# Another order of the tensors in SBUF: the arena of hidden rows ahead of constants and split activations

## The reference

```python
def first_block(...):
    proj = rmsnorm(h, g) @ w_in                  # q, k, v, u, y
    h += concat(dilated attention, bidirectional RG-LRU) @ w_out
    h += cross attention to 256 memory rows      # w_cq, w_ck, w_cv, w_co
    hid = square(relu(rmsnorm(h, g) @ w_mlp_in)) # 1024 x 4096
    h += hid @ w_mlp_out                         # 4096 x 1024
    return rmsnorm(h, g)

def second_block(...):                           # two layers
    z = rmsnorm(x) @ w_in                        # four branches and four gates
    x += (gated sum of MLA, FNet, differential attention, HGRN2) @ w_out
    x += (silu(g) * u) @ w_down                  # w_gate_up: 1024 x 5632, w_down: 2816 x 1024
```

## Time and profile before

| | |
|---|---|
| median of 3 runs | 1296.85 us (1294.33 to 1297.41) |
| the profiled execution | 1295.53 us |
| its span, first to last instruction | 1293.7 us |
| TensorE matmul busy | 1265.9 us (98%) |
| TensorE weight loads busy | 1178.1 us (91%) |
| VectorE busy | 862.2 us (67%) |
| ScalarE busy | 652.5 us (50%) |
| GpSimd busy | 114.4 us (9%) |
| granted TensorE clock, mean | 0.994 |

### The profile page before, as it was taken

How to read it: one execution, slowest core, us unless ns; L and a number is a source line. 1 busy time by engine, 2 the same in 40 slices (tenths; PEclk the granted TensorE clock), 3 DMA queues, 4 the chain that set the end, 5 groups by cost and what they waited for, 6 DMA issues and landing times.

```text
span 1293.7 us, 22072 instructions
## 1 busy us (share of the span) xinstructions
PE 1265.9 (98%) x9208; PEld 1178.1 (91%) x9208; DVE 862.2 (67%) x1194; ACT 652.5 (50%) x1049; POOL 114.4 (9%) x152
## 2 busy tenths in 40 slices
PE   8999999999999999998999999999999999999998
PEld 8998999988788989997999998888899988999986
DVE  6897667644466675998656553667577996655543
ACT  5896655543368464342544443556552434544432
POOL 1100000000000000661000000000003810000000
PEclk8999999999999999999999999999999999999999
DMA  9543445555535323442555555433343325455552
GB/s 368 204 163 115 180 135 192 196 185 180 188 101 193 131 99 131 164 152 84 189 189 176 190 196 185 165 139 136 112 145 131 134 96 196 165 191 174 187 196 98
DMA packets 30324, 211.77 MB, mean 164 GB/s; under 512 B 3344, under 2 KB 3728, under 8 KB 5264
## 3 DMA queue, kind: packets, MB, share of 16 engines
q1 hardware_dynamic: 29936, 210.22, 45.5%
q10 hardware_dynamic: 288, 0.14, 0.0%
HBM read 209.29 MB, written 1.05 MB: 163 GB/s over the span
## 4 chain that ended last, share of the span: by engine, by line
PE 74%; DVE 13%; ACT 6%; issue 5%; DMA 1%; SPq 0%; DVEq 0%; ACTq 0%
PE bank L508 72%; DVE w_lo L1625 3%; ACT w_hi L1125 2%; DVE W L1599 2%; DMA ring<-weight_pieces 1%; ACT W L1125 1%; PE bank L608 1%; PE bank L843 1%; DVE xs L2125 1%; DVE W L1585 1%; DVE junk L2123 1%; DVE W L2105 1%; DVE W L1586 1%; DVE W L1617 0%; DVE stat L1558 0%
## 5 line engine op out<-in xcount | busy, mean ns | idle before, releaser
L1625 DVE TENSOR_TENSOR w_lo<-ring,w_hi 128x2048 fp32r<-128x2048 f32 x183 | 422.5, 2309 | 283.9 <-ACT w_hi L1125 283.5
L1125 ACT ACTIVATE w_hi<-ring 128x1024 fp32r<-128x1024 f32 (+1 forms) x368 | 366.2, 1046 | 241.9 <-PE bank L508 226.2
L508 PE MATMUL bank<-x_hi,w_hi 128*128 128x256 f32 x1840 | 267.2, 284 | 2.4 <-ACT w_hi L1125 2.4
L508 PE MATMUL bank<-x_hi,w_lo 128*128 128x256 f32 x1840 | 261.5, 281 | 1.0 <-DVE w_lo L1625 0.9
L508 PE MATMUL bank<-x_lo,w_hi 128*128 128x256 f32 x1840 | 254.8, 280 | 0.0
L508 PEld LDWEIGHTS bank<-x_hi,w_hi 128*128 128x128 f32 x1840 | 237.0, 189 | 5.7 <-issue 2.4
L508 PEld LDWEIGHTS bank<-x_hi,w_lo 128*128 128x128 f32 x1840 | 236.5, 188 | 2.3 <-DVE w_lo L1625 1.7
L508 PEld LDWEIGHTS bank<-x_lo,w_hi 128*128 128x128 f32 x1840 | 233.6, 188 | 0.0
L508 PE MATMUL bank<-W 128*128 128x128 f32 (+4 forms) x716 | 110.7, 327 | 8.3 <-ACT W L1125 4.8
L508 PEld LDWEIGHTS bank<-W 128*128 128x128 f32 (+3 forms) x716 | 87.8, 187 | 21.5 <-issue 12.3
L508 PE MATMUL bank<-w_lo,hid_hi 128*128 128x512 f32 x304 | 78.5, 394 | 0.0
(11 more groups left out here) (257 smaller groups left out, 1238.0 us busy)
## 6 DMA issues: line engine op xcount, KB each, us to landing
ring<-weight_pieces SPq DMA_DIRECT2D x191, 1024.0 KB, 4.8
const<-constants SPq DMA_DIRECT2D x1, 1376.5 KB, 8.9
W<-x_features SPq DMA_DIRECT2D x4, 256.0 KB, 5.2
ring<-weight_pieces SPq DMA_DIRECT2D x2, 512.0 KB, 6.0
h<-x SPq DMA_DIRECT2D x2, 512.0 KB, 11.9
W<-rg_weights SPq DMA_DIRECT2D x1, 1024.0 KB, 9.7
xs<-mem_features SPq DMA_DIRECT2D x1, 1024.0 KB, 11.4
oT<-mem SPq DMA_DIRECT2D x1, 1024.0 KB, 11.4
```

Of the source, the lines that this page charges most:

```text
L508: return nc.tensor.matmul(out, lhsT, rhs, start=first, stop=last)
L1125: return nc.scalar.activation(out, in_, ACT.Copy, scale=scale)
L1625: v.tensor_tensor(w_lo[:, q % SPLITS, 0:n], raw(pp)[:, 0:n], w_hi[:, q % SPLITS, 0:n].bitcast(F32), ALU.subtract).then_inc(s_weight_low, 1)
```

## The change

Four groups of allocations change their order; nothing else does. Before: `ring`, `w_hi`, `w_lo`, `const`, `vec`, `row`, `h`, `xs`, `x_hi`, `x_lo`, `oT`, `W`, `junk`, ... After: `ring`, `w_hi`, `w_lo`, `h`, `xs`, `oT`, `W`, `const`, `vec`, `row`, `x_hi`, `x_lo`, `junk`, ... So `ring`, `w_hi`, `w_lo`, `junk`, `stat` and `rrow` stay where they are, and all others move. The arena with the hidden rows starts 57,344 bytes behind the start of `w_hi`, a multiple of 1024.

```diff
         w_hi = sb("w_hi", [P, SPLITS, PIECE], F32R)
         w_lo = sb("w_lo", [P, SPLITS, PIECE], F32R)
-        const = sb("const", [P, C_SIZE])
-        vec = sb("vec", [P, V_SIZE])
-        row = sb("row", [P, R_SIZE])
         h = sb("h", [P, TT, D])
         xs = sb("xs", [P, TT, D])
-        x_hi = sb("x_hi", [P, KT, S], F32R)
-        x_lo = sb("x_lo", [P, KT, S], F32R)
         oT = sb("oT", [P, KT, S])
         W = sb("W", [P, ARENA])
         arena0 = nc.sbuf_base - 4 * ARENA
...
         mem_lo = nc.alloc_sbuf_tensor_at("mem_lo", [P, KT, S], F32R, offset=arena0 + 4 * A_U)
+        const = sb("const", [P, C_SIZE])
+        vec = sb("vec", [P, V_SIZE])
+        row = sb("row", [P, R_SIZE])
+        x_hi = sb("x_hi", [P, KT, S], F32R)
+        x_lo = sb("x_lo", [P, KT, S], F32R)
         junk = sb("junk", [P, D], BF16)
```

## The result

The changed kernel takes 1300.56 us (median of 5, 1299.92 to 1301.06), the kernel before 1294.91 us (median of 5, 1293.5 to 1297.41): ratio **1.0039**, 95% interval 1.0027 to 1.0051. It is slower by 0.4%. The forecast was no change, 1296.5 us.

What follows compares the result with a forecast made beforehand. TensorE's matmul count times start-to-start pace was taken as the bound, 996 of 1293.7 us. All terms of the change were taken as 0, giving 1296.5 us, between 1295.53 (profiled) and 1296.85 (median); range 1271 to 1309.

Steps and rivals of the forecast that it cites:

- Other engines: Accesses of engines besides TensorE to the moved tensors: covered by the matmuls, no row making their effect other than 0.
- the feature matmuls, 192 to 160: 5520 matmuls with activations moving, remainder by 512 from 192 to 160: pace stays at 117.8 ns, 0 us.
- the bound above, +26 us: Upper limit for the 5520 feature matmuls: one more step like 113 to 118 ns, +4.8 ns each.
- rival C: Slower, equal or off-line places collide more: feature +4 us, token +3, hidden rows +2.4, total 1306 us; chance 0.26.
- Token matmuls, 320 to 352: 1152 matmuls with weights moving and activations stationary, remainder by 512 from 320 to 352: taken as 0 us.
- the bound above, +3 us: Upper limit for the 1152 token matmuls: all at 118 ns, instead of half at 113 and half at 118.
- Down matmuls, 320 to 0: 912 matmuls of 512 columns on hidden rows, remainder 320 to 0: stay at 233.3 ns, 0 us; bounds -16 and +6.
- rival B: Only the down stage gets faster, 224 to 228 ns, -5 to -8 us, 1290 us; chance 0.15 including small feature gains.
- The remark on mem_hi: Memory rows mem_hi, at a multiple of 128, were the slower of their pair; given on the down term's open sign.
- C's parts on feature and token matmuls: Slower case's terms: feature matmuls +0.7 ns each, +4 us; token matmuls always at 118 ns, +3 us.
- C's part on the hidden rows: Slower case's term for the down matmuls: 236 ns, which a pass could reach by 1%, +2.4 us.
- C's reason: Slower case's mechanism: TensorE's moving read and weight load meet at the same place more often.

Runs made afterwards that it cites:

- e1: Kernel before, with 32 unused bytes ahead of x_hi and 480 ahead of W, so only the split activations change remainder; ratio 1.0073, 1305.15 us.
- e2: Kernel before, with 192 unused bytes ahead of W, so only the hidden rows change remainder, to 0; ratio 0.993, 1287.16 us.
- e3: Kernel before, with 32 unused bytes ahead of ring, so every tensor from ring on shifts and all distances stay; ratio 1.0004.
- e4: Kernel before, with 384 unused bytes ahead of x_hi and 64 ahead of W, exchanging feature and token remainders; ratio 0.9916, 1285.07 us.
- a2: Changed kernel with 480 unused bytes ahead of x_hi, restoring the activations' old remainder; ratio 0.9963 to the kernel before, 1290.24 us.
- a1: Changed kernel with 96 unused bytes ahead of x_hi, feature remainder 64; ratio 0.9908 to the kernel before, 1283.09 us.
- s3: Kernel before, with 128 unused bytes ahead of x_hi and 96 ahead of W: feature remainder 64, hidden rows 32; ratio 0.9972.
- s1: Kernel before, with 192 unused bytes ahead of x_hi and 128 ahead of W: feature remainder 0, hidden rows 128; ratio 1.0091, 1305.94 us.

## Why the prediction was wrong

**What held.** TensorE sets the time, the number of matmuls times their pace carries 77% of the span, and the only question was whether the remainders of the distances count. The distances and remainders worked out from the sizes were right, and so was the suspicion that the remainder and not the distance matters. (They are those from the start of the moving tensor to that of the stationary one; the text names the opposite direction.) Other engines: 0, as forecast. The range held the time.

**Step that failed: the feature matmuls, 192 to 160, "I take 0".** It interpolated between two rows, 128 (memory rows, 118.0 ns) and 192 (117.8). Remainder 160 lies between them and has 119.94. Two things were wrong in it. The pace isn't a smooth function of the remainder, so neighbours don't bound a place between them. And the 118.0 ns wasn't the pace of 128: 24 of the 56 memory matmuls move mem_lo, which is at 192. The next row of mem_hi alone had 118.8, and the activations at 128 settle at 118.76, so the two neighbours differ by 1.0 ns and not by 0.2. The term was +12.0 us by pace, +9.5 in the distances of the traced executions, half of that difference by the clock; the bound above, +26 us, held it. The text gave +0.7 ns to rival C; it was +2.2, outside the 117.1 to 118.5 ns that the prediction had named as the limits for its being right.

**Token matmuls, 320 to 352, "I take 0".** The loss of the lower level was the bound above, +3 us; it happened, as 118.27 against 115.24 ns, 3.5 us by pace. Only 0.7 of it is left in the traced executions: 1.4 us is the half clock, 1.2 the step to `w_lo`.

**Down matmuls, 320 to 0, "I take 0".** This is what rival B forecast, in size too: 226.8 ns where 224 to 228 was named, -6.0 us. The reason given for 0, that two products with different steps both paced at 233.3, was empty: both have the remainder 320, and only steps that are multiples of 512 differed. It was one place seen twice. The remark on mem_hi, slower at a multiple of 128, pointed the wrong way for 512 columns.

So B came true together with C's parts on feature and token matmuls, with opposite signs (C's part on the hidden rows, +2.4 us, did not), and I had them as alternatives. The chances should not have been taken apart so: the parts concern different pairs of tensors, and any of them can come with any other. C's reason, that equal places collide more, isn't shown: equal places (0) are slow for 256 columns and fast for 512.

**The rule that TensorE never waits on anyone** (the Trainium skill, SBUF — State Buffer, "Who interferes with whom") would have given exactly 0. The runs show no waiting for another engine, but the time isn't independent of where TensorE's own two operands lie: e1 and e2 differ from the kernel before in nothing but the places of tensors, and the feature pace of e1 changes by +1.8%, the down pace of e2 by -2.8%. What in the chip takes the time isn't shown; that it hangs on both operands is, since e3 moves both and nothing changes.

**Open.** Why one and the same place settles at 113 or at 118 ns after a wait (before at 320, e4 at 320, e2 and a2 at 192), and what lies behind the period of 256 bytes. No run separates the moving read from the weight load. Where two levels occur, the time varies more too: a1's four executions take 1279.34 to 1287.36 us and s3's eight 1287.75 to 1295.82, those of the changed kernel 1299.92 to 1301.06. Whether the share of the lower level changes from one execution to the next isn't shown, as one of each was traced.

## What to carry to other kernels

Where dense float32r matmuls follow each other, work out for every pair of operands the distance between their starts by 256 bytes and measure a few values: here paddings of 32 to 480 bytes moved the kernel before by -0.8% (e4) to +0.9% (s1), and the changed kernel by -1.3% (a1), with no other edit. When a change only reorders allocations, treat each pair's new remainder as unmeasured, give each pair a price and a chance of its own, and don't interpolate between remainders. Take a pace from starts and counts (the chain's xcount over its time), not from mean durations: 280 against 282 ns hid a step of 2.2 ns in 118.

## What was not expected of the hardware

The start-to-start distance of float32r matmuls depends on the distance between moving and stationary operand by 256 bytes: 113.3 to 119.9 ns for 256 columns, 226.7 to 234.3 ns for 512. For 256 columns 64 was best, for 512 columns 0; what is worst for the one (0 and 160, 119.9 ns) is at 0 best for the other. At some remainders (64, 192) a stretch settles at one of two levels, 113.3 or 117.8 ns, and keeps it until the next long distance or matmul of another form: in the kernel before, e2, e4, a1, a2 and s3 none of the 51 stretches of 16 or more steady feature matmuls changed level, in e3 one did. fp32 matmuls at half rate showed none of it: the 256-column ones of oT and ring start 215.9 ns apart at remainder 192 (before) and at 0 (after).
